# Stick-breaking attention with queries on partitions, a reversed scan on VectorE, and log weights turned by TensorE

## The reference

```python
z = jnp.einsum('bqhd,bkhd->bhqk', q, k) * HEAD_DIM ** -0.5 + b_sb   # per head
mask = k_pos[None, :] < q_pos[:, None]                               # strictly causal
log_keep = jnp.where(mask, jax.nn.log_sigmoid(-z), 0.0)
after = lax.cumsum(log_keep, axis=3, reverse=True) - log_keep        # sum over later keys
a = jnp.where(mask, jnp.exp(jax.nn.log_sigmoid(z) + after), 0.0)
o = jnp.einsum('bhqk,bkhd->bqhd', a, v)
```

## Time and profile before

| | us |
|---|---|
| median of three runs | 977.85 |
| lowest, highest | 975.02, 979.13 |
| the profiled execution | 981.96 |
| span of its trace | 980.2 |
| third group in it, from slot 8 to the next group's slot 8 | 194.6 |

### The profile page before, as it was taken

The page is one execution under the profiler, slowest core; times in us unless marked ns, Lnnn a source line. Parts: engine busy times, 40 slices in busy tenths (PEclk is TensorE's granted clock), DMA queues, the critical chain, the costliest instruction groups (busy, mean ns, idle before and its releaser), DMA issues.

```text
span 980.2 us, 15526 instructions
## 1 busy us (share of the span) xinstructions
PE 887.8 (91%) x3961; PEld 501.5 (51%) x3961; DVE 594.9 (61%) x853; ACT 370.9 (38%) x721; POOL 407.6 (42%) x234
## 2 busy tenths in 40 slices
PE   1899987899999879999999899999997999999996
PEld 0556744445675544455765444567554445534442
DVE  2443789885436697854357988633679875322334
ACT  6211354763202546632026475320264753121122
POOL 1007455673073646730746477207364772010000
PEclk9989999999999999999999999999999999989999
DMA  9967536466278764663777646647866566565101
GB/s 329 332 218 258 157 118 197 158 215 214 100 234 253 231 202 145 213 195 111 236 246 248 198 166 196 194 131 235 263 213 215 163 192 226 193 216 169 69 22 45
DMA packets 128052, 189.11 MB, mean 193 GB/s; under 512 B 9680, under 2 KB 50685, under 8 KB 127952
## 3 DMA queue, kind: packets, MB, share of 16 engines
q1 hardware_dynamic: 96752, 172.27, 53.8%
q10 hardware_dynamic: 31200, 15.73, 5.7%
HBM read 179.49 MB, written 8.49 MB: 192 GB/s over the span
## 4 chain that ended last, share of the span: by engine, by line
PE 37%; issue 26%; POOL 21%; SPq 8%; DMA 4%; DVE 2%; POOLq 1%; ACT 0%; DVEq 0%; ACTq 0%
PE ps L1095 37%; POOL prod L483 19%; SPq L346 3%; SPq L338 3%; POOL later_lo L490 3%; DMA ring<-in_w_ada_dram 2%; DMA ring<-in_cache_k_dram 1%; SPq L306 1%; DMA hT<-in_w_out_dram 1%; DVE zd L953 0%; POOLq L480 0%; DMA ring<-in_cache_v_dram 0%; DVE zb L819 0%; DVE sp_lo L885 0%; DVE qb L808 0%
## 5 line engine op out<-in xcount | busy, mean ns | idle before, releaser
L1095 PE MATMUL ps<-hT,wsl 128*128 128x344 f32 x1344 | 431.5, 463 | 2.3 <-issue 2.3
L483 POOL TENSOR_TENSOR prod<-ring,qb 128x1024 f32<-128x1024 f32 x128 | 311.0, 2437 | 233.6 <-DVE qb L808 156.8
L1095 PEld LDWEIGHTS ps<-hT,wsl 128*128 128x128 f32 x1344 | 249.1, 192 | 142.4 <-issue 32.7
L953 DVE TENSOR_REDUCE zd<-prod 128x16 f32<-128x1024 f32 x128 | 155.0, 1211 | 40.4 <-POOL prod L483 40.4
L512 ACT ACTIVATE sp<-sp 128x512 f32<-128x512 f32 (+3 forms) x192 | 100.5, 524 | 157.3 <-DVE sp L867 153.7
L490 POOL TENSOR_TENSOR later_lo<-later,later_hi 128x512 fp32r<-128x512 f32 (+3 forms) x80 | 87.0, 1087 | 163.0 <-ACT later_hi L512 162.9
L867 DVE TENSOR_SCALAR sp<-ps,bsb 128x512 f32<-128x512 f32 (+3 forms) x96 | 58.8, 612 | 88.7 <-PE ps L1095 88.1
L885 DVE TENSOR_TENSOR sp_lo<-sp,sp_hi 128x512 fp32r<-128x512 f32 (+3 forms) x96 | 65.2, 679 | 19.7 <-ACT sp_hi L512 18.5
L1095 PE MATMUL ps<-ring,apad 128*8 128x512 f32 x512 | 69.7, 613 | 6.9 <-DMA ring<-in_cache_v_dram 6.9
L1095 PE MATMUL ps<-hT,xy 128*128 128x512 f32 x160 | 73.3, 601 | 1.3 <-DMA hT<-in_w_out_dram 1.2
L873 DVE SCALAR_TENSOR_TENSOR sp<-ps,bsb,sp 128x512 f32<-128x512 f32 (+3 forms) x96 | 59.1, 616 | 18.8 <-ACT sp L512 17.8
(11 more groups left out here) (218 smaller groups left out, 831.9 us busy)
## 6 DMA issues: line engine op xcount, KB each, us to landing
ring<-in_cache_k_dram SPq DMA_DIRECT2D x256, 256.0 KB, 2.9
ring<-in_cache_v_dram SPq DMA_DIRECT2D x256, 256.0 KB, 2.9
wsl<-in_w_in_dram ACTq DMA_DIRECT2D x30, 512.0 KB, 5.2
ring<-in_w_ada_dram SPq DMA_DIRECT2D x6, 2048.0 KB, 12.0
xy<-in_x_prompt_dram SPq DMA_DIRECT2D x2, 2048.0 KB, 10.6
out_dram<-oT SPq DMA_DIRECT2D x8, 512.0 KB, 3.7
ring<-in_x_prompt_dram SPq DMA_DIRECT2D x8, 512.0 KB, 7.7
hT<-in_w_out_dram SPq DMA_DIRECT2D x5, 512.0 KB, 6.8
```

Source lines behind the costliest of these rows:

```text
L483: pool.tensor_tensor(prod[:, t % 2].rearrange("p (j c) -> p j c", j=2), kring[:, t % 4], qb[:, t // 16].unsqueeze(1).to_broadcast([P, 2, H ...
L953: v.tensor_reduce(zd[:, t // 16, :, r:r + 2], prod[:, t % 2].rearrange("p (j h d) -> p h j d", j=2, h=NH), AX_X, ALU.add)\
L1095: return nc.tensor.matmul(out, l, r, start=start, stop=stop, skip_group_check=True)
```

## The change

The attention unit is turned around: 128 queries on partitions, up to 512 keys along the free dimension.

- `UNITS` now goes by blocks of 128 queries. Query block `t` below 4 is one part of `t + 1` key blocks; a later one is two parts: the last four key blocks, then the first `t - 3`. There are 24 units as before, of key blocks 1, 2, 3, 4, 4, 1, 4, 2, 4, 3, 4, 4, each for two heads.
- `scores` swaps the operands and uses two banks, one for each head; it waits until both units before have left them.
- DVE writes `min(z + b, 40)` to `zc` (three buffers). ACT writes `relu(z + b - 40)` to `rise`, and Exp and Ln of `zc` to `sp`. So softplus is `rise` plus `sp`, with `rise` of a key taken one column further on.
- DVE `log_weights`: one `tensor_tensor_scan` with reversed operands sums `rise` and `sp` from the last key to the first, started from `carry` where the query's later keys were another unit; a second instruction subtracts the sums from `zc`. The second waits for the first on `scan_done`. L873, L885 and `add_later` are gone, as are ACT's two rounding copies and POOL's L490.
- PE `turn` transposes the log weights, block by block, to a single bank `TB`; ACT `weights` takes Exp of it to `av`. `turn(u)` waits for `weights` of the unit before. `suffix` is gone.
- `outputs` multiplies block by block: one matmul of 128 columns for each key block and head.
- A projection unit still has four blocks of the contraction in the even slot and four in the odd one (`EVEN_KS`), now in one piece behind `turn`.
- Once in a group the last two columns of `ub` are copied (`last2`) by a reversed scan of two columns; once in the kernel `bsh` and two constants are written.

The core of the diff:

```diff
-UNITS = [(c, i, h) for c in range(2) for i in range(4 * c + 3, -1, -1) for h in range(2)]
+PARTS = [(t, 0, t + 1) for t in range(4)]
+for t in range(4, TT):
+    PARTS += [(t, t - 3, 4), (t, 0, t - 3)]
+UNITS = [(t, b0, nb, h) for t, b0, nb in PARTS for h in range(2)]
...
+EVEN_KS = 4
...
         @block.gpsimd
-                    if t - 10 in RUPD:
-                        u = t - 10
-                        pool.wait_ge(later_hi_ready, len(RUPD) * g + RUPD.index(u) + 1)
-                        pool.tensor_tensor(later_lo[:, first_col(u):QC], later[:, UNITS[u][2], first_col(u):QC],
-                                           later_hi[:, first_col(u):QC], ALU.subtract).then_inc(later_lo_ready, 1)
...
         @block.scalar
+            def weights(g, u, first):
+                act.wait_ge(lwT_full, NU * g + u + 1)
+                if not (first and u < 4):
+                    act.wait_ge(pv_done, NU * g + u - 3)
+                run(av[:, u % 4, 0:P * UNITS[u][2]], ps[:, TB, 0:P * UNITS[u][2]], ACT.Exp, a_ready)
...
+                        if u >= 2 and u % 2 == 1:
+                            weights(g, u - 2, first)
                         act.wait_ge(zc_ready, NU * g + u + 1)
-                        run(z, z, ACT.Exp, exp_done)
+                        if not (first and u < 2):
+                            act.wait_ge(lw_ready, NU * g + u - 1)
+                        run(rise[:, u % 2, lo:QC], ps[:, Z + u % 2, 0:QC - lo], ACT.Relu, rise_ready,
+                            bias=bsh[:, bass.ds(2 * g + head, 1)])
+                        z = sp[:, u % 2, lo:QC]
+                        run(z, zc[:, u % 3, lo:QC], ACT.Exp, exp_done)
                         act.wait_ge(exp_done, NU * g + u + 1)
                         run(z, z, ACT.Ln, ln_done, bias=1.0)
...
+                    if u >= 2 and u % 2 == 0:
+                        weights(g, u - 2, first)
...
         @block.vector
+                    if u >= 1 and u % 2 == 0:
+                        log_weights(g, u - 1, first)
                     if u >= 0:
+                        lo, h = first_col(u), UNITS[u][3]
                         v.wait_ge(z_full, NU * g + u + 1)
+                        if not (first and u < 3):
+                            v.wait_ge(lwT_full, NU * g + u - 2)
+                        v.tensor_scalar(zc[:, u % 3, lo:QC], ps[:, Z + u % 2, 0:QC - lo],
+                                        bsb[:, bass.ds(2 * g + h, 1)], CLAMP, ALU.add, ALU.min).then_inc(zc_ready, 1)
+                    if u >= 1 and u % 2 == 1:
+                        log_weights(g, u - 1, first)
                     if t > 0:
                         reduce_pair(g, t - 1)
-                    if u >= 0:
-                        v.wait_ge(ln_done, NU * g + u + 1)
-                        v.scalar_tensor_tensor(sp[:, u % 2, lo:QC], ps[:, Z + u % 3, lo:QC], ...
...
+                v.tensor_tensor_scan(back(sums[:, par_, lo:QC]), back(rise[:, par_, lo + 1:QC + 1]),
+                                     back(sp[:, par_, lo:QC]), start, ALU.add, ALU.add).then_inc(scan_done, 1)
+                v.wait_ge(scan_done, NU * g + u + 1)
+                if u in CARRIES:
+                    v.tensor_tensor(carry[:, h:h + 1], sums[:, par_, 0:1], rise[:, par_, 0:1], ALU.add)\
+                        .then_inc(carry_ready, 1)
+                v.tensor_tensor(zc[:, u % 3, lo:QC], zc[:, u % 3, lo:QC], sums[:, par_, lo:QC], ALU.subtract)\
+                    .then_inc(lw_ready, 1)
...
         @block.tensor
                     if not (first and u == 0):
-                        pe.wait_ge(a_ready, NU * g + u - 1)
+                        pe.wait_ge(zc_ready, NU * g + u)
+                        pe.wait_ge(rise_ready, NU * g + u)
...
+                def turn(u):
+                    lo, nb = first_col(u), UNITS[u][2]
+                    pe.wait_ge(lw_ready, NU * g + u + 1)
+                    if not (first and u == 0):
+                        pe.wait_ge(a_ready, NU * g + u)
+                    for j in range(nb):
+                        last = nc.tensor.transpose(ps[:, TB, P * j:P * (j + 1)],
+                                                   zc[:, u % 3, lo + P * j:lo + P * (j + 1)], ident[:, :])
+                    last.then_inc(lwT_full, 1)
...
-                        project(m, part, chunk, ks[0:2])
+                        ks = range(0, EVEN_KS) if u % 2 == 0 else range(EVEN_KS, KT)
+                        project(m, GC_ + (m - 9) // 3, (m - 9) % 3, ks)
-                    if 1 <= u <= NU:
-                        suffix(u - 1)
-                    if u < NU:
-                        project(m, part, chunk, ks[2:4])
```

More of the change, by code:

```diff
@@ L125, in stick_breaking_mixer @@
         sp = sb("sp", [P, 2, QC])
-        sp_hi = sb("sp_hi", [P, 2, QC], F32R)
-        sp_lo = sb("sp_lo", [P, 2, QC], F32R)
+        zc = sb("zc", [P, 3, QC])
+        rise = sb("rise", [P, 2, QC + 1])
+        sums = sb("sums", [P, 2, QC])
+        carry = sb("carry", [P, 2])
+        bsh = sb("bsh", [P, NH])
+        last2 = sb("last2", [P, 2])
+        naught = sb("naught", [P, 2])
         av = sb("av", [P, 4, QC])
-        later = sb("later", [P, 2, QC])
-        later_hi = sb("later_hi", [P, QC], F32R)
-        later_lo = sb("later_lo", [P, QC], F32R)
         qsP = sb("qsP", [P, HALF])
@@ L399, in _ @@
             load_wo(WO_ORDER[0])
-            sp_e.wait_ge(lo_ready, NU * GROUPS)
+            sp_e.wait_ge(scan_done, NU * GROUPS)
             load_wo(WO_ORDER[1])
@@ L623, in body @@
                     if 0 <= u < NU:
-                        lo, z = first_col(u), sp[:, u % 2, first_col(u):QC]
+                        lo, head = first_col(u), UNITS[u][3]
+                        if u >= 2 and u % 2 == 1:
+                            weights(g, u - 2, first)
                         act.wait_ge(zc_ready, NU * g + u + 1)
-                        run(z, z, ACT.Exp, exp_done)
+                        if not (first and u < 2):
[4 more added lines that the diff above has]
+                        run(z, zc[:, u % 3, lo:QC], ACT.Exp, exp_done)
                         act.wait_ge(exp_done, NU * g + u + 1)
                         run(z, z, ACT.Ln, ln_done, bias=1.0)
-                    if 1 <= u <= NU:
[L630 to L644, removed]
+                    if u >= 2 and u % 2 == 0:
+                        weights(g, u - 2, first)
                     if t < 8:
@@ L662, in body @@
                         decode_a(g, 0, first)
+                evac(g, first, last, 21)
+                weights(g, NU - 1, first)
                 decode_ln(g, 1)
-                evac(g, first, last, 21)
                 evac(g, first, last, 22)
@@ L912, in body @@
                         decode_log_weights(0)
+                log_weights(g, NU - 1, first)
                 reduce_pair(g, SLOTS - 1)
@@ L1107, in _ @@
             last.then_inc(par_full, 1)
[L1110 removed]
+            pe.wait_ge(dve_const, 14)
             pe.wait_ge(cT_copied, 1)
@@ L1307, in body @@
                     page_values(t)
+                    if u < NU and u % 2 == 0:
+                        scores(u)
+                    if u >= 2:
+                        turn(u - 2)
                     if u < NU:
[L1309 to L1310 removed]
                         m = 9 + u // 2
[L1312 to L1314 removed]
+                        ks = range(0, EVEN_KS) if u % 2 == 0 else range(EVEN_KS, KT)
+                        project(m, GC_ + (m - 9) // 3, (m - 9) % 3, ks)
                     else:
                         project(21 + u - NU, BC_, u - NU)
[L1317 to L1320 removed]
                     if t == 19:
```

122 lines of the change are left out of this document (44 added, 78 removed).

## The result

The changed kernel takes 1005.98 us (median of four runs, 1003.6 to 1012.49) against 976.91 for the kernel before (four runs, 975.02 to 979.13): ratio 1.0307, interval 1.025 to 1.0364. It is slower, by 29 us in the medians. The medians of the kernel before, which ran again beside each set of experiments, lie between 976.91 and 980.03, so a difference of a few microseconds between versions of different sets is near what such medians can tell apart.

The account below looks back on a forecast made before the run. DVE and POOL taking turns were to bound the attention: 12.3 us more a group less 3.2 back, times 4, is 36 on 981.96, 1018 profiled, less 4.1, 1014 us; range 940 to 1075, likeliest case 990 to 1045.

Parts of the forecast that it names:

- The held instructions: DVE in a full pair: scan held in odd slot (5.51 us), subtraction in even slot (5.73), pair 11.2.
- The handover: DVE between scan and subtraction: a handover on a semaphore of 0.16 us.
- The other two-tensor instructions and latencies: DVE per group: SiLU pairs 4.8 us, decode softmax 3.4, carries 0.8, others 0.6, together 9.6; latencies 3.
- The scan: DVE's scan of 512 columns: 1.22 us with a per-column surplus; 0.96 if fixed, 1.38 if the whole doubles.
- The Trainium skill's rule on word pairs: DVE's reversed read of `rise`, one word off: a full scan would be 1.47 us, the time some 18 more.
- PE in time: PE in a full pair: 8.6 us of work, ready at 7.7, wanted by DVE at 9.4, spare 1.7.
- The sign that was named wrongly: PE waiting for `zc`, listed among what would show the forecast right; no size given.
- The tail: PE behind slot 31: 16.7 us behind the last reduce against 19.9 before, 3.2 back in each group.
- PE stays the bound: Rival: scan runs beside the product, PE's order decides; full pair 9.6 to 9.7 us, 908 us, chance 0.18.
- DVE keeps its turn: Rival: even-slot subtraction passes before the waiting product; full pair 9.6 to 9.9 us, 950 us, chance 0.12.
- The dearer scan: Rival, on DVE: half a scan more, 1.75 us, gives 1052 us; range with the clock 1045 to 1110, chance 0.14.
- The clock, its other half: Same rival, PE: granted clock falls, deciding only under 0.8; at 1.2 GHz a full pair gains 4 us; shared chance 0.14.

Follow-up runs that it names:

- Experiments 1 and 2: Product cut to 64 of 1024 elements: changed kernel 910.9 us, kernel before 943.43; product made to wait for log weights: changed kernel 943.52, kernel before (for `sp_lo`) 978.73.
- Experiment 4: Changed kernel with ACT doing `weights(u-2)` ahead of Relu, Exp and Ln in even slots too: 999.72 us (1.0209).
- before_product_later: Kernel before, with POOL's product t also waiting for `sp_lo` of the unit of t - 9: 978.73 us (0.9989).

## Why the prediction held, point by point

The forecast was 1014 with a range of 940 to 1075; the time is 1006. The mechanism is the one named. Of the 36 us summed for the profiled execution, 22.1 came. From first PSUM read to last reduce the four groups are longer by 10.5, 5.5, 8.5 and 8.6 us, 33.1 in all, where the sum has 4 x 12.3 = 49.2; the stretches behind them give back 9.2, where it has 12.8; and the first group starts 1.8 us sooner, within what that start varies by (105.3 to 107.6 us in the traces of all runs). So the attention's lengthening was put too high by half. That 1014 and 1006 lie as near as 8 us is in part luck: between the medians the two kernels lie 29 us apart, between the profiled executions only 22.1.

- **The held instructions.** Predicted: odd slot 5.51, even slot 5.73, full pair 11.2. The trace has 5.44 (621.45 to 626.89), 5.68 (to 632.57), 11.12. By the sum the subtraction of an even slot is held by 1.94 us (its end at 3.93 instead of 1.99). This stands in the carry's 2.12, or in the subtraction where there is no carry (546.49, 2.66 us instead of 0.69). Experiments 1 and 2 show that the product is the cause. The product's own time in even slots was put too high, 3.20 in this pair against 3.4 to 3.6. The Trainium skill (VectorE: DVE Perf Modes, Two Vector instructions with no wait between them) has instructions with two SBUF tensors read through an interface shared with GpSimd; the carry's 2.12 us for one column agrees with it.
- **The handover was mis-sized.** 0.16 us was taken between scan and subtraction, from the earlier trace rows. The rows above have 0.03 (624.97 to 625.00). In the third group the sum was 3.8 us too large (135.6 against 131.8). The fifteen slots that hold nothing beside the reduce, the PSUM read and the log weights end 0.11 us earlier each than the formulas say, 1.6 of the 3.8.
- **The other two-tensor instructions and latencies.** Put at 9.6 + 3 = 12.6. The other nine slots are longer than the formulas by 10.5, so 2.1 less, the rest of the 3.8; in one of them 0.73 is a wait for PE's scores (619.57). One reason is that a held instruction pays the wait for the one behind it: with `zb` held to 2.20 us at 551.46, the scan at 554.69 ran at its own 1.21.
- **The scan.** The prediction took 1.22 for 512 columns, and the trace has 1.22 where it runs free (626.81). The per-column reading of the earlier trace rows was right: 1.01 for 384 columns (615.26) and 0.48 for 128 (573.75), with the carry as start, which adds 0.06 at 512 (637.86, 1.28). The timeline of DVE in the changed kernel:

```profile
545.24 1.22 DVE L964 TENSOR_TENSOR_SCAN sums<-rise,sp 128x512 f32<-128x512 f32 x1
546.49 2.66 DVE L970 TENSOR_TENSOR zc<-zc,sums 128x512 f32<-128x512 f32 x1
...
573.75 0.48 DVE L964 TENSOR_TENSOR_SCAN sums<-rise,carry,sp 128x128 f32<-128x128 f32 x1
...
637.86 1.28 DVE L964 TENSOR_TENSOR_SCAN sums<-rise,carry,sp 128x512 f32<-128x512 f32 x1
```

- **The Trainium skill's rule on word pairs.** By the Trainium skill (Vector Engine (DVE) Microarchitecture Reference, 5.2), a stream that starts one word off would have made this 1.47, an estimate. The rows disagree: 1.22, so neither the odd start of `rise` nor the negative step cost anything beside the scan's own pace. The measurement decides for this instruction; a scan takes about twice as long for a column as the subtraction, so a slower stream may be hidden in it. (That a negative step was not measured stands in 5.1 of that page, not in 5.2.)
- **PE in time.** Its work in a full pair was priced at 8.6 us. From the starts in its timeline (622.84 on): turns 0.39 and 0.50, half projections 2.41 and 2.40, outputs 0.80, values 0.99, scores 1.06: 8.55. `outputs` in pieces of 128 columns cost no more than the old form, as taken. The timeline of PE in the changed kernel:

```profile
622.84 0.55 PE L1253 MATMUL ps<-ident,zc 128*128 128x128 f32 x3 [0.82 <-ACT av L512]
623.23 2.48 PE L1092 MATMUL ps<-hT,wsl 128*128 128x344 f32 x8
625.64 0.88 PE L1092 MATMUL ps<-av,vN 128*64 128x128 f32 x12
626.44 1.06 PE L1092 MATMUL ps<-ring,apad 128*8 128x512 f32 x8
627.43 1.13 PE L1092 MATMUL ps<-kT,qT 64*128 64x512 f32 x4
628.49 0.66 PE L1253 MATMUL ps<-ident,zc 128*128 128x128 f32 x4
628.99 2.48 PE L1092 MATMUL ps<-hT,wsl 128*128 128x344 f32 x8
```

- **The sign that was named wrongly.** PE was said to wait for `zc`. The profile puts the wait down to ACT's `av`, since ACT's `weights` came last before `turn`; ACT in turn waits 214.5 us for DVE (L512 rise <-DVE zc L870). Experiment 4 shows that DVE stands behind it. With ACT's order changed the attention is no shorter (530.4 against 531.2 us), so the spare time that was worked out for PE held there.
- **The tail.** Predicted 3.2 us back in a group, from the last reduce to PE's next projection. In the third group these are 623.04 to 642.95 before, 19.9 us, and 641.00 to 659.03 after, 18.0: only 1.9 back. Before each of these projections PE idles with no releaser that the profile shows, 1.04 and 0.96 us; the 19.9 holds this gap, the 25.3 worked out for after does not.
- **The rivals.** "PE stays the bound" at 908 needed a scan that runs beside the product; it doesn't, but with the product cut to 64 elements the kernel takes 910.9, so the price of that case was near and its condition false. "DVE keeps its turn" fell on the carry of 2.12 us: a gap of 0.03 us between scan and carry was enough for the waiting product. The dearer scan fell on 1.22. The clock, its other half, is there but small: where PE had waited 4.14 us for ACT, its granted clock was 0.64 over the next 4.1 us, between its two levels of 1.2 and 2.4 GHz, and half a projection took 3.62 us instead of 2.48. The timeline of PE there:

```profile
611.55 1.11 PE L1253 MATMUL ps<-ident,zc 128*128 128x128 f32 x4 [4.14 <-ACT av L512]
612.46 3.62 PE L1092 MATMUL ps<-hT,wsl 128*128 128x344 f32 x8
```

And the row of that stretch by windows, with the columns of the earlier trace rows:

```profile
611.80:615.90 4.10, 4.10 (x12) 2.58 (x11) 4.07 (x4) 2.00 (x4) 1.49 (x2) 0.64 0.80 214
```

DVE waited only 0.73 us for PE behind it (619.57), so the dip cost about that in this group, far from the 31 us by which the range of that rival starts above the forecast.

## What to carry to other kernels

Before moving work to VectorE, look at what GpSimd runs beside it: count the instructions that read two SBUF tensors, because those take turns with GpSimd's, whole instruction by whole instruction, and a one-column one can wait two microseconds. Count copies from SBUF to SBUF too: the last section shows one that was held. If they must share a slot, choose when the GpSimd instruction starts, by a wait on the VectorE result behind which only PSUM reads and reduces stand; here that wait was worth 62 us of 1006, more than the whole change. A wait put on one instruction of a double-buffered pair should be put on both: on one alone the two run back to back, and of the 62 us only 46 or 6 were gained.

## What was not expected of the hardware

- VectorE and GpSimd **alternate**: when a two-tensor instruction of VectorE ends, the waiting product goes first, even with VectorE's next one 0.03 us behind. A product of 2.36 us that started 0.16 us after the scan ended 2.14 us behind the scan's end, so its first 0.2 us seem to run beside the other engine's instruction.
- **Two tensors are not the whole condition.** The reduces and the instructions that read PSUM keep their times, but the copy of 128 columns from `sp` to `later` in the kernel before, with one SBUF tensor read, took 0.22 us alone and 2.34 beside a product that ended at 546.64; its mean of 0.584 over 56 copies comes to about 20 us held in that kernel. In the changed kernel a `tensor_scalar` from `zb` to `zx` (256 columns, 0.29 us alone) took 2.33 once. No run tells which one-tensor instructions are concerned. The timelines of POOL and of DVE in the kernel before:

```profile
544.28 2.36 POOL L483 TENSOR_TENSOR prod<-ring,qb 128x1024 f32<-128x1024 f32 x1 [2.21 <-DVE zd L953]
...
544.38 2.34 DVE L970 COPY later<-sp 128x128 f32<-128x128 f32 x1
...
550.92 0.22 DVE L970 COPY later<-sp 128x128 f32<-128x128 f32 x1
```

- The scan reads two tensors backwards, one of them starting one word off, at 1.22 us for 512 columns of fp32, about twice a plain two-tensor instruction (0.69), and 0.48 for 128.
- The kernel before does not gain from the same care (0.9989), although the product costs it 35 us. There VectorE is held less (busy 578.8 us instead of 594.9), and the time stays. In before_product_later the new wait was the last to end for only 20 products of 128; `later_lo` still waits 153.5 us for ACT, and holds back the products behind it:

```profile
POOL later_lo L492 <- ACT later_hi L514: 153.5, 76, 8.4
...
POOL prod L485 <- DVE sp_lo L887: 53.7, 20, 9.6
```

The lines are of the view of waits (us in total, times, longest us).
